# Attention by head pairs in halves of the array, with denominators from a ones product

## The reference

```python
def diff_attn(q1, q2, k1, k2, v, lam):          # kind B, 4 heads, two halves of 32
    p1 = jax.nn.softmax(einsum(q1, k1) * scale, axis=-1)
    p2 = jax.nn.softmax(einsum(q2, k2) * scale, axis=-1)
    return einsum(p1 - lam * p2, v)

# na_latent (kind A, 4 heads of 64): 2-D neighbourhood with a learned bias, plus 512 cached keys
# swa_latent (kind D, 4 query heads, 2 key heads): band of 3 x 128 keys, plus 512 cached keys, plus a sink logit
p = jax.nn.softmax(jnp.concatenate([s_loc, s_ctx], axis=-1), axis=-1)
out = einsum(p_loc, v_loc) + einsum(p_ctx, v_ctx)
```

## Time and profile before

| what | us |
|---|---|
| median of 3 runs | 3991.99 |
| lowest, highest | 3991.58, 3994.47 |
| span of the profiled execution | 3990.3 |
| PE busy (18444 products) | 3818.4, 96% |
| PEld busy | 2987.1, 75% |
| DVE busy | 2073.6, 52% |
| ACT busy | 916.8, 23% |
| POOL busy | 571.4, 14% |

### The profile page before, as it was taken

How to read it: one execution, slowest core, us unless ns; L and a number is a source line. 1 busy time by engine, 2 the same in 40 slices (tenths; PEclk the granted TensorE clock), 3 DMA queues, 4 the chain that set the end, 5 groups by cost and what they waited for, 6 DMA issues and landing times. The chain is left out here.

```text
span 3990.3 us, 47296 instructions
## 1 busy us (share of the span) xinstructions
PE 3818.4 (96%) x18444; PEld 2987.1 (75%) x18444; DVE 2073.6 (52%) x3428; ACT 916.8 (23%) x1718; POOL 571.4 (14%) x446
## 2 busy tenths in 40 slices
PE   6899999899999999999989989999999999999998
PEld 4787556565888888888868865566668888888886
DVE  5222555555376666666573235555546455555555
ACT  3111455444110000000031125544522000000002
POOL 0011111101211111111131111110122111111112
PEclk8999999999999999999989989999999999999999
DMA  6754323563221221122215433255450101110011
GB/s 226 232 178 135 76 52 79 131 155 115 85 74 49 74 74 64 48 74 74 65 53 183 134 95 83 51 128 130 114 175 32 32 32 43 43 43 32 32 43 53
DMA packets 289646, 358.53 MB, mean 90 GB/s; under 512 B 102994, under 2 KB 215508, under 8 KB 289296
## 3 DMA queue, kind: packets, MB, share of 16 engines
q1 hardware_dynamic: 269008, 350.54, 30.1%
q10 hardware_dynamic: 20416, 4.98, 0.6%
HBM read 288.28 MB, written 72.16 MB: 90 GB/s over the span
## 5 line engine op out<-in xcount | busy, mean ns | idle before, releaser
L2068 PE MATMUL bank<-h_hi,w_hi 128*128 128x512 f32 (+1 forms) x2496 | 906.0, 363 | 18.8 <-issue 14.7
L2069 PE MATMUL bank<-h_lo,w_hi 128*128 128x512 f32 (+1 forms) x2496 | 886.3, 355 | 0.0
L2070 PE MATMUL bank<-h_hi,w_lo 128*128 128x512 f32 (+1 forms) x2496 | 886.2, 355 | 0.0
L2225 PE MATMUL bank<-prob,vv 128*128 128x512 f32 (+3 forms) x1504 | 703.4, 549 | 0.0
L1886 DVE SCALAR_TENSOR_TENSOR xT<-bank,mods,xT 128x512 f32<-128x512 f32 (+1 forms) x816 | 533.3, 659 | 269.3 <-PE bank L2070 257.2
L2068 PE MATMUL bank<-m_hi,w_hi 128*128 128x512 f32 (+1 forms) x1536 | 555.2, 361 | 17.0 <-DVE xT L1886 16.8
L2070 PE MATMUL bank<-m_hi,w_lo 128*128 128x512 f32 (+1 forms) x1536 | 549.1, 357 | 0.0
L2068 PEld LDWEIGHTS bank<-h_hi,w_hi 128*128 128x128 f32 x2496 | 473.5, 190 | 100.9 <-issue 33.7
L2069 PE MATMUL bank<-m_lo,w_hi 128*128 128x512 f32 (+1 forms) x1536 | 548.9, 357 | 0.0
L1761 DVE TENSOR_REDUCE mp<-bank 128x1 f32<-128x512 f32 (+1 forms) x576 | 377.8, 659 | 294.0 <-PE bank L2171 292.9
L2069 PEld LDWEIGHTS bank<-h_lo,w_hi 128*128 128x128 f32 x2496 | 473.8, 190 | 73.2 <-issue 7.7
(11 more groups left out here) (188 smaller groups left out, 4077.4 us busy)
## 6 DMA issues: line engine op xcount, KB each, us to landing
stage<-in_w_mlp SPq DMA_DIRECT2D x64, 1024.0 KB, 5.2
nx_w<-in_w_ada SPq DMA_DIRECT2D x16, 1536.0 KB, 9.2
stage<-in_w_in SPq DMA_DIRECT2D x18, 1024.0 KB, 6.3
ada_h<-in_w_ada SPq DMA_DIRECT2D x16, 1024.0 KB, 8.4
rope_t<-in_k_rope SPq DMA_DIRECT2D x28, 512.0 KB, 4.6
k<-s_kB SPq DMA_DIRECT2D x48, 224.0 KB
k<-s_kA SPq DMA_DIRECT2D x24, 448.0 KB, 10.5
k<-s_kD SPq DMA_DIRECT2D x24, 448.0 KB, 10.5
```

Of the source, the lines that this page charges most:

```text
L2068: x = pe.matmul(out, a_hi, b_hi, start=first, stop=False)
L2069: pe.matmul(out, a_hi, b_lo, start=False, stop=False)
L2070: return x, pe.matmul(out, a_lo, b_hi, start=False, stop=last)
L2225: pe.matmul(ob[:, q0:q0 + n], vv[h % 2][:, key0 // P], prob[si % NP_RING][:, :n], start=(i == 0 and kind != "D"), stop=(i == len(steps) - ...
```

## The change

- Jobs are pairs of heads: 8 v instead of 16 (B, B, B, B, A, D, A, D), 24 jobs, STEPS 188. Each step does both heads x = 0, 1.
- `values`: two products with 64 stationary columns each, whose outputs are the halves 0 to 63 and 64 to 127 of the partitions of one bank. There are no ones columns.
- `scores` in B: two full products with 97 rows, as before one after the other. In A and D: q and k of both heads lie in the two halves of 64 rows; three products per head (hi hi, lo hi, hi lo) and one that adds the negative maximum, the two heads in turn. `piece` in A and D takes row halves too. Units u = 2s + x use banks 2 to 4 in turn.
- Denominators: GpSimd adds the probabilities of both heads (`add_step`), in B over four steps, in A, D and the small chunks over the job; one product with ones for each head, in column halves of bank 7 (`sums`), four steps later. ScalarE copies them (`take_sum`), SyncE takes them to DRAM job by job.
- Banks 0 and 1 hold the pieces of the two heads, and the maximum rows as well: `max_row` and `piece` wait for each other.
- The ring of probabilities has four pairs; it also waits for GpSimd's adds.
- `load_head`, `load_values` and the second `load_bias` are issued by ScalarE (the first head and the first bias by SyncE). The output ring ao_hi/ao_lo has two buffers instead of three. The Fourier tables are loaded in the last head pair.

```diff
-    jobs, v = [], 0
-    for kind, heads in (("B", [(h, s) for h in range(4) for s in range(2)]), ("A", [(h, 0) for h in range(4)]),
-                        ("D", [(h, 0) for h in range(4)])):
-        for h, s in heads:
-            for c in range(NCH):
-                jobs.append((kind, h, s, c, v))
-            v += 1
+    jobs = []
+    for v, (kind, h2, s) in enumerate((("B", 0, 0), ("B", 0, 1), ("B", 1, 0), ("B", 1, 1),
+                                       ("A", 0, 0), ("D", 0, 0), ("A", 1, 0), ("D", 1, 0))):
+        for c in range(NCH):
+            jobs.append((kind, h2, s, c, v))
...
+def sum_groups():
+
+    gs = []
+    for j, (kind, _, _, c, _) in enumerate(JOBS):
+        n, g = n_steps(j), SUM_STEPS if kind == "B" and c < 2 else n_steps(j)
+        gs += [(j, i, min(i + g, n)) for i in range(0, n, g)]
+    return gs
+
+
+SUM_STEPS, SUM_LAG = 4, 4
+SUMS = sum_groups()
+NSUM = len(SUMS)
+SUM_FIRST = {j: g for g, (j, i0, _) in enumerate(SUMS) if i0 == 0}
+SUM_LAST = {j: g for g, (j, _, i1) in enumerate(SUMS) if i1 == n_steps(j)}
+SUM_AT = [STEP0[j] + i1 - 1 + SUM_LAG for j, _, i1 in SUMS]
+SUM_OF = {STEP0[j] + i: g for g, (j, i0, i1) in enumerate(SUMS) for i in range(i0, i1)}
...
+VALUES_OF = [0, 0, 1, 1, 2, 3, 4, 5]
+VALUES_FIRST = [v == 0 or VALUES_OF[v] != VALUES_OF[v - 1] for v in range(NV)]
+HEAD_DMAS = [{"B": 12 + 2 * (v < 2), "A": 2, "D": 3}[JOBS[v * NCH][0]] for v in range(NV)]
...
+RECIP_AT = [STEP0[(v + 1) * NCH] + 8 for v in range(NV - 1)]
+SCALE_AT = [STEP0[(v + 1) * NCH] + 12 for v in range(NV - 1)]
...
+BIAS1_AT = STEP0[5 * NCH] + 2
+LOADS_AT = {STEP0[v * NCH] + 1: v + 1 for v in range(1, NV - 1)}
+VALUES_AT = {STEP0[v * NCH] + 4: v + 1 for v in range(1, NV - 1) if VALUES_FIRST[v + 1]}
...
-    NP_RING = 5
+    NP_RING = 4
     prob = []
     for s in range(NP_RING):
-        a, off = at(f"prob{s}", [P, 512], F32, off)
+        a, off = at(f"prob{s}", [P, 2, 512], F32, off)
...
+    def score_bank(u):
+        return 2 + u % 3
...
+    def load_head(e, l, v):
+
+        kind, h2, half, _, _ = JOBS[v * NCH]
+        b = v % 2
+        if v >= 2:
+            e.wait_ge(s2_full, l * 2 * STEPS + 2 * STEP0[(v - 1) * NCH])
+        S, R = head_in[b], rest_in[b]
+        if kind == "B":
+            for x, (q, k) in enumerate(((q1[b], k1[b]), (q2[b], k2[b]))):
+                r0 = (2 * h2 + x) * 64 + half * 32
+                for row, pq, pk in ((0, 0, 0), (32, 1, 0), (64, 0, 1)):
+                    e.dma_start(q[row:row + 32].bitcast(F32), s_q["B"][pq, r0:r0 + 32]).then_inc(S, 16)
+                    e.dma_start(k[row:row + 32].bitcast(F32), s_k["B"][pk, r0:r0 + 32]).then_inc(S, 16)
...
+            def add_step(s):
+
+                j, i = STEP_JOB[s]
+                _, q0, n, _ = key_steps(JOBS[j][0], JOBS[j][3])[i]
+                g = SUM_OF[s]
+                total = acc[g % 2][:, :, q0:q0 + n]
+                pool.wait_ge(p_rdy, l * 2 * STEPS + 2 * s + 2)
+                if opens_sum(s - 1):
+                    if g >= 2:
+                        pool.wait_ge(den_full, l * NSUM + g - 1)
+                    pool.tensor_tensor(total, prob[(s - 1) % NP_RING][:, :, :n], prob[s % NP_RING][:, :, :n], ALU.add
+                                       ).then_inc(p_add, 1)
+                else:
+                    pool.wait_ge(p_add, l * NADDED + ADDED[s] - 1)
+                    pool.tensor_tensor(total, total, prob[s % NP_RING][:, :, :n], ALU.add).then_inc(p_add, 1)
+
+            for s in range(STEPS):
+                if s in SCALE_AT:
+                    scale(SCALE_AT.index(s))
+                if not opens_sum(s):
+                    add_step(s)
+            scale(NV - 1)
...
+                    act.wait_ge(p_add, l * NADDED + ADDED[si - NP_RING])
+                    settle(act)
+                for x in range(2):
...
+            load_head(act, l, 1)
             max_row(0)
...
+                if s == BIAS1_AT:
+                    act.wait_ge(s1_max, l * 2 * PIECES + 2 * PIECE0[5 * NCH])
+                    settle(act)
+                    act.wait_ge(s2_add, l * 2 * NADD + 2 * ADD0[5 * NCH])
+                    settle(act)
+                    load_bias(act, l, 1)
+                if s in LOADS_AT:
+                    load_head(act, l, LOADS_AT[s])
+                if s in VALUES_AT:
+                    load_values(act, l, VALUES_AT[s])
...
+                for x in range(2):
+                    if pieces_out[0]:
+                        pe.wait_ge(s1_max, l * 2 * PIECES + 2 * pieces_out[0] - 1 + x)
+                    if kind == "B":
+                        q, k = pair_operands(j)[x]
+                        rows = slice(0, 96)
+                    else:
+                        q, k, rows = q1[b], k1[b], slice(64 * x, 64 * x + 64)
+                    pe.matmul(bank[:, x, :n], q[rows, q0:q0 + P], k[rows, key0:key0 + n], start=True, stop=True
+                              ).then_inc(s1_full, 1)
+                pieces_out[0] += 1
...
                 pe.wait_ge(m_col, l * NJ + j + 1)
                 if j:
-                    pe.wait_ge(m_rdy, l * NJ + j)
+                    pe.wait_ge(m_rdy, l * M_ROW0[NJ] + M_ROW0[j])
+                pe.wait_ge(s1_max, l * 2 * PIECES + 2 * pieces_out[0])
                 for t in range(CHUNKS[c][1] // P):
-                    mm = pe.matmul(bank[:, 7, t * P:(t + 1) * P], mcol[j % 2][:, t:t + 1].to_broadcast([P, P]), ident_r,
-                                   start=True, stop=True)
+                    for x in range(2):
+                        mm = pe.matmul(bank[:, x, t * P:(t + 1) * P], mcol[j % 2][:, x, t:t + 1].to_broadcast([P, P]),
+                                       ident_r, start=True, stop=True)
                 mm.then_inc(m_rowp, 1)
+                rows_out[0] = j + 1
...
+            def bank_free(u):
+
+                j, i = STEP_JOB[u // 2]
+                if (j, i) in ADD_INDEX:
+                    pe.wait_ge(s2_add, l * 2 * NADD + 2 * ADD_INDEX[(j, i)] + u % 2 + 1)
+                else:
+                    pe.wait_ge(p_rdy, l * 2 * STEPS + u + 1)
 
...
+                out = [bank[:, score_bank(2 * si + x), :n] for x in range(2)]
+                for x in range(2):
+                    if 2 * si + x >= 3:
+                        bank_free(2 * si + x - 3)
+                    if kind == "B":
+                        q, k = pair_operands(j)[x]
+                        pe.matmul(out[x], k[0:97, ks], q[0:97, qs], start=True, stop=True).then_inc(s2_full, 1)
                 if kind == "B":
-                    mm = pe.matmul(out, k1[b][0:97, k], q1[b][0:97, q], start=True, stop=True)
-                else:
-                    pe.matmul(out, k1[b][:, k], q1[b][:, q], start=True, stop=False)
-                    mm = pe.matmul(out, k2[b][:, k], q2[b][:, q], start=False, stop=True)
-                mm.then_inc(s2_full, 1)
+                    return
+                for y, (k, q) in enumerate(((k1[b], q1[b]), (k1[b], q2[b]), (k2[b], q1[b]))):
+                    for x in range(2):
+                        rows = slice(64 * x, 64 * x + 64)
+                        pe.matmul(out[x], k[rows, ks], q[rows, qs], start=(y == 0), stop=False)
+                for x in range(2):
+                    rows = slice(64 * x, 64 * x + 64)
...
+                pe.wait_ge(p_rdy, l * 2 * STEPS + 2 * si + 2)
+                for x in range(2):
+                    f = slice(0, HD) if kind == "D" else slice(x * HD, (x + 1) * HD)
+                    mm = pe.matmul(bank[64 * x:64 * x + 64, 5 + j % 2, q0:q0 + n], vv[VALUES_OF[v] % 2][:, key0 // P, f],
+                                   prob[si % NP_RING][:, x, :n], start=(i == 0), stop=(i == len(steps) - 1))
+                mm.then_inc(pv_done, 1)
+
+            def sums(g):
+
+                j, i0, i1 = SUMS[g]
+                kind, _, _, c, _ = JOBS[j]
+                n = CHUNKS[c][1]
+                pe.wait_ge(p_add, l * NADDED + ADDED[STEP0[j] + i1 - 1])
+                first = g == SUM_FIRST[j]
+                if first and j:
+                    pe.wait_ge(den_ev, l * NJ + j)
+                if kind == "D":
+                    pe.wait_ge(sink_p, l * len(D_JOBS) + D_JOBS.index(j) + 1)
+                    settle(pe)
+                    for x in range(2):
+                        pe.matmul(bank[64 * x:64 * x + 64, 7, :n], sink_rows[:, x], p_sink[:, :n], start=True, stop=False)
+                for x in range(2):
+                    mm = pe.matmul(bank[64 * x:64 * x + 64, 7, :n], ones[:, 0:HD], acc[g % 2][:, x, :n],
+                                   start=(first and kind != "D"), stop=(g == SUM_LAST[j]))
+                mm.then_inc(den_full, 1)
...
                     if s in ROW_AT:
                         max_row(ROW_AT.index(s))
-                if s >= LAG:
+                if LAG <= s < STEPS + LAG:
                     values(*STEP_JOB[s - LAG])
-            pe.wait_ge(s1_max, (l + 1) * PIECES)
+                if s in SUM_AT:
```

(5 more changed lines are left out.)

522 lines of the change are left out of this document (258 added, 264 removed).

## The result

The changed kernel takes 4091.24 us (median of 4; 4089.95 to 4093.4), the kernel before 3991.78 on the same chip: a ratio of 1.0247, interval 1.0233 to 1.0262. The forecast was 3974, its range ended at 4085.

A forecast was written before the change was run, and what follows sets the result against it. TensorE was taken to bound B fully, and A and D except for about 41 us of waits. Per layer B -6, A and D -25, ends +22 gave -9, -18 in all: 3974 us, range 3890 to 4085.

The forecast's parts named there:

- Products: TensorE's product time per layer with both kinds of halves overlapping: 202 us in B, 153 in A and D.
- Rivals 3 and 5: 3: row halves in A and D don't overlap, 4104, chance .06; 5: column halves don't overlap, 4328, chance .04.
- Restarts: Each pair step's change of tiling and back: .40 us in B, .50 in A and D; 42 us each per layer.
- Rival 1: Restarts cost more at the 188 pair steps per layer, a slowdown: at .25 us more, 4068; chance .25.
- Row waits: Row products wait 1.4 us for VectorE's reductions of the pieces: 17 us in B, 9 in A and D.
- two-piece steps: Steps with two or more piece pairs wait within themselves, 15 x .7 and one of 3: 13 us, A and D.
- ScalarE's issues: Exponentials stand behind DMA issues on ScalarE: 3 us twice in B; 13 in A and D, 8 of it bias.
- the 10 deducted: In A and D, 10 us per layer taken off since a wait covers part of a drain.
- The sum of before: Old kernel per layer from product prices: B 269 us against 272.5 measured; A and D 220 against 261, 41 waiting.
- The ends: Start and end of attention, 22 us per layer: prologue pieces 12.6, first head's load 3, last sums 3, output ring 3.
- GpSimd: Additions of 1024 in attention take 2.4 us, hidden; VectorE's work there (second kind: PSUM and SBUF inputs) doesn't block them.
- The signs: Tests of failure: B's period, row-half score pairs over .25 us, exponentials waiting for GpSimd, over 100 us waits in A, D.

The follow-up runs named there:

- e6: Changed kernel with throwaway products in the waits before second pairs of pieces and before row products; ratio 1.0225 to the kernel before.
- e12: e11 with four more edits: first reciprocals before bias tables, SyncE loads values, stores two steps apart, some pieces earlier; ratio .9954 to the kernel before.
- e8: Changed kernel with second and later pairs of pieces moved behind the step's values in steps without row products; ratio 1.0176 to the kernel before.
- e1: Changed kernel with SyncE's Fourier loads issued before the last denominators and stores; ratio 1.0188 to the kernel before.
- e15: Changed kernel with GpSimd's running additions cut to 8 of 512 columns per head; ratio 1.0252 to the kernel before.
- e11: Changed kernel with Fourier loads earlier, 12 piece pairs ahead, row products and second pairs behind values, ScalarE's issues spread; ratio 1.0016 to the kernel before.
- e7: Changed kernel with throwaway products in the prologue alone; ratio 1.0236 to the kernel before.

## Why the prediction was wrong

Point by point, for layer 0, by the forecast's own steps.

- **Products.** 202 and 153 us, with both kinds of halves overlapping: right. The value pairs, the score slots and the sums measured as drawn (2.14 and 2.26 us per step). Rivals 3 and 5 are out.
- **Restarts.** .36 and .37 in place of .40 and .50: 37 + 31 = 68 us, where 84 stood in the sum. Wrong by 16 us in the change's favour. Rival 1, the one I gave most, was not what happened.
- **Row waits, two-piece steps, ScalarE's issues.** The places and the releasers were as forecast. In B 17 + 6 us were expected; TensorE stood 19.5 (274.6 - 255.1): 2.98 and 2.79 for ScalarE, and .82 to 1.46 at each of the twelve row waits where 1.4 was taken. In A and D the forecast's terms came to 33 net of the 10 deducted; it stood 45.9 (260.5 - 214.6), of which 7.79 for the bias issues (8 forecast).
- **The clock.** The step that failed most. The sum of before set "about 41 us of A and D is waiting", without the .94 in the same row: TensorE stood 23.5 us there, and 10 more were the lower level. The forecast then added new waits to a stream that never had any in B and priced them at their own length. Behind some of them, four of the fifteen in B, products ran at the lower level: 11 us lacking in B for 3 (2 of the 8 more come from the prologue's level and not from waits), 26 in A and D for 10, so 24 us per layer that no term held. With it the sum closes: B 202 + 37 + 19.5 + 11 = 269.5 (measured 274.6), A and D 153 + 31 + 8 + 46 + 26 = 264 (260.5). The 5 us open in B have a forerunner: the sum of before gave 269 for 272.5, and the forecast set its 267 beside the 272.5, so the 3.5 unexplained were dropped. That the waits cause the low clock is shown for B (e6). For A and D it is not: e12 took away waits and low clock together, e8 waits alone, and the cause there stays open.
- **The ends.** The prologue was forecast well (+15.3 for 12.6, and +5.4 for 3). The end was not: +18.2 for 6, the second step that failed. "After the last step the last sums come before the Fourier part starts" was true and small; SyncE's queue, in which the Fourier loads come behind stores that depend on steps 183 to 185, was never walked to its end. e1 prices it at 12 and 10 us per layer.
- **GpSimd.** 2.4 us was forecast for an addition of 1024, 2.37 measured; hidden, as said (e15). "VectorE's work in attention is of the second kind" was misread: the subtraction `ao_lo` has both inputs in SBUF, and it took up to 2.53 us beside these additions. But the text looked only at its throughput, and not at what a late scale does to the exponentials' ring (e11).

- **The signs.** "Wrong if a period of B differs from 2.4 by over .2" is met by the plain step, 2.14, though the forecast's own prices give 2.18 for it; 2.4 is the mean with a sum (.86) every fourth step, and there 2.36 was measured (469.73 to 479.15, four steps). The sign was badly drawn, and the step was right.

In us per layer: A and D missed by 32, the end by 12, B by 7, the start by 5. Some 7 of the 32 are only the yardstick: the 261 us of before ran from 682 to 943, while its A and D last from 683.4 to 937.4. That the gaps and the low clock are the loss is borne out by e12, which leaves 24 of the 46 us that TensorE stood in A and D and 7 of the 20 in B, and comes to 3976; that this is near the 3974 forecast for the kernel as written proves nothing for the forecast. Not followed: the first piece of layer 1 is 54.2 us late, 8 more than the 46 of the table, of which layer 1's own start may hold 5.

## What to carry to other kernels

When an engine that never waits gets its first short waits, allow for the time that it may run at its lower clock behind them (in B 7 us for 19.5 us of waits), and read the clock column of the old trace before calling anything a wait. Walk each queue to the stage's last instruction, not only through the loop: what stands behind an item that depends on the last steps is late by construction. And put any product whose input comes from a slower engine behind the largest block of independent work in its step; here two such moves were worth 28 us each.

## What the hardware showed beyond what was expected

- A change of tiling costs .35 to .37 us for a round trip between full and column halves (2.14 against 1.79 us) or row and column halves (2.26 against 1.89 of products). The way back to row halves is no cheaper from full than from column halves (1.05 against 1.01).
- TensorE's clock fell to 1.2 GHz behind a single wait of 2.98 us, in B also behind 1.46 and 1.23, and in A behind 1.30; but waits of 1.24 and 1.25 in B (busy 7.51 of 10 us, 480 to 490) left it at 1.00. 28.39 busy of 30 us in e7's prologue didn't raise it from .50, and in after the first 8 us of B, busy throughout, ran at .50 as well.
- VectorE's subtraction of 512 columns with both inputs in SBUF took 2.53 us beside a GpSimd addition, .68 without. The Trainium skill, SBUF — State Buffer, Who interferes with whom, describes the two engines' shared ports as an exclusive lock; the forecast used it only for GpSimd's side, and it is VectorE that was held.
